# Low halves of the input projection's weight chunks 4 to 14: from VectorE to GpSimd

## The reference

```
h = rmsnorm(x, norm1_g) * (1 + sc1) + sh1
q_m, k_m, v_m, o_m, gate_m, conv_in, cq_raw, ckv_raw, krope = split_in(h @ p['w_in'])
y_m = mlstm_mixer(...)      # chunkwise matrix memory, forward and backward
y_c = conv_module(...)      # gated, then a depthwise convolution 31 wide, LayerNorm, pointwise
y_a = attention over latent queries and keys (8 heads)
x = x + g1 * (concat(y_m, y_c, y_a) @ p['w_out'])
x = x + g2 * ffn(rmsnorm(x) ...)
```

## Time and profile before

| | |
|---|---|
| median of 3 runs | 3638.81 us |
| profiled execution | 3644.04 us, its span 3642.20 us |
| PE busy | 3385.1 us (93%) |
| DVE busy | 1878.8 us (52%) |
| ACT busy | 864.7 us (24%) |
| POOL busy | 321.7 us (9%) |
| mean granted clock of TensorE | 0.95 of full |

### The profile page before, as it was taken

One profiled execution on the slowest core, in us unless ns is written; L12 is line 12 of the kernel. 1 busy time (PEld: TensorE's weight loads), 2 busy tenths in 40 slices (PEclk: granted clock), 3 DMA queues, 4 the chain that ended last, 5 costly groups with the idle time before them and its releaser, 6 DMA issues. The chain is left out here.

```text
span 3642.2 us, 45449 instructions
## 1 busy us (share of the span) xinstructions
PE 3385.1 (93%) x18642; PEld 3020.9 (83%) x18642; DVE 1878.8 (52%) x3068; ACT 864.7 (24%) x1332; POOL 321.7 (9%) x276
## 2 busy tenths in 40 slices
PE   5989989999899999999989896999997999999998
PEld 4988856557789999999979885655586999999998
DVE  6694644444666556565366655444415434433343
ACT  3212334444221111011132223344422111111100
POOL 0000111222110000000010001122121000000000
PEclk7996879999999999999999888899998999999999
DMA  5210100003322222122021000000110111111111
GB/s 246 88 32 1 62 4 4 3 12 122 106 75 76 86 75 81 63 83 80 28 87 45 18 3 16 2 4 3 45 66 32 50 35 46 35 46 46 46 35 53
DMA packets 44805, 185.60 MB, mean 51 GB/s; under 512 B 5440, under 2 KB 8960, under 8 KB 43136
## 3 DMA queue, kind: packets, MB, share of 16 engines
q1 hardware_dynamic: 37760, 158.58, 12.5%
q0 software_dynamic: 6912, 25.17, 2.4%
HBM read 169.14 MB, written 14.59 MB: 50 GB/s over the span
## 5 line engine op out<-in xcount | busy, mean ns | idle before, releaser
L1103 PE MATMUL ps<-a_hi,gu_hi 128*128 128x384 f32 x2112 | 711.9, 337 | 30.4 <-DVE a_lo L1630 24.2
L1103 PE MATMUL ps<-a_lo,gu_hi 128*128 128x384 f32 x2112 | 710.1, 336 | 0.0
L1103 PE MATMUL ps<-a_hi,gu_lo 128*128 128x384 f32 x2112 | 710.0, 336 | 0.0
L1103 PEld LDWEIGHTS ps<-a_hi,gu_hi 128*128 128x128 f32 x2112 | 400.0, 189 | 36.8 <-issue 18.0
L1103 PEld LDWEIGHTS ps<-a_lo,gu_hi 128*128 128x128 f32 x2112 | 400.1, 189 | 0.0
L1103 PEld LDWEIGHTS ps<-a_hi,gu_lo 128*128 128x128 f32 x2112 | 400.0, 189 | 0.0
L1132 PE MATMUL ps<-g_hi,d_hi 128*128 128x384 f32 x1056 | 354.3, 336 | 4.3 <-DVE g_lo L2081 4.3
L2079 DVE TENSOR_TENSOR at<-ps,sg 128x384 f32<-128x384 f32 x132 | 73.4, 556 | 545.9 <-ACT sg L1511 545.9
L1132 PE MATMUL ps<-g_lo,d_hi 128*128 128x384 f32 x1056 | 354.2, 335 | 0.0
L1132 PE MATMUL ps<-g_hi,d_lo 128*128 128x384 f32 x1056 | 353.9, 335 | 0.0
L1980 DVE TENSOR_REDUCE pmx<-ps 128x1 f32<-128x384 f32 (+1 forms) x400 | 213.4, 543 | 235.5 <-PE ps L1003 235.2
(11 more groups left out here) (261 smaller groups left out, 5095.2 us busy)
## 6 DMA issues: line engine op xcount, KB each, us to landing
f_raw<-wgu SPq DMA_DIRECT2D x88, 512.0 KB, 4.4
diag<-wada_c POOLq DMA_DIRECT2D x48, 512.0 KB, 3.8
f_raw<-wdn SPq DMA_DIRECT2D x44, 512.0 KB, 4.4
w_raw<-win SPq DMA_DIRECT2D x32, 512.0 KB, 3.6
spill<-z SPq DMA_DIRECT2D x2, 4608.0 KB
z<-spill SPq DMA_DIRECT2D x2, 4608.0 KB, 13.6
w_raw<-wout SPq DMA_DIRECT2D x16, 512.0 KB, 4.0
wada_o<-wada_b SPq DMA_DIRECT2D x16, 512.0 KB, 3.7
```

What stands on the lines that cost most here:

```text
L1103: mm = MM(ps[:, 2 * (v % 2) + part, 0:BLK], w, a[:, k, b * BLK:(b + 1) * BLK], start=(k == 0 and j == 0), stop=(k == KC - 1 and j == 2))
```

## The change

Eleven calls of `w_low` leave VectorE's list and stand as a loop in GpSimd's, behind its `a_lo` and in front of its `kw`. Chunks 0 to 3 and 15 stay on VectorE. The same subtraction is made on the same operands, with the same semaphores.

```diff
@@ VectorE
                 gated(0)
                 if l == 0:
                     late_modulation(0, 2)
-                w_low(4)
                 if l == 0:
                     late_modulation(2, 5)
-                w_low(5)
                 gated(1)
...
                 taps(0, 4)
-                w_low(6)
                 taps(4, 7)
                 kr_rows(0)
-                w_low(7)
                 dve.wait_ge(ml_reset.sem, ml_reset.at(l, 16))
                 gates()
                 scans(fw, False)
                 kr_rows(1)
-                w_low(8)
                 scans(bw, True)
                 row_maxima()
-                w_low(9)
                 row_offsets()
                 kr_rows(2)
                 taps(7, 9)
-                w_low(10)
                 taps(9, 13)
-                w_low(11)
                 taps(13, 17)
-                w_low(12)
                 taps(17, 21)
-                w_low(13)
                 taps(21, 22)
                 dve.wait_ge(ml_dmm.sem, ml_dmm.at(l, 1))
...
                 taps(22, 26)
-                w_low(14)
                 taps(26, CONV_WIDTH)
@@ GpSimd
                 low_halves(0)
+                for n in range(4, 15):
+                    w_low(n)
```

## The result

The changed kernel takes 3718.55 us, the median of four runs (3715.46 to 3721.61), and the kernel before, beside it, 3638.88 us (3636.89 to 3642.09). The ratio is 1.0218, with a 95% interval from 1.0200 to 1.0236. The forecast of 3633.9 us and its range are wrong. It came out as the fourth rival said, which gave about 3700 us and had a chance of 0.02.

A forecast was written before the change was run, and what follows sets the result against it. TensorE is 93% busy, but VectorE's chain was taken to end the stage; 2.44 us gained a layer, 4.9 us in both, turns 3644.04 into 3639.1, or 3633.9 us on the median's footing 5.2 us lower. Range 3628 to 3641.

The forecast's parts named there:

- the fourth rival: GpSimd doesn't get in between VectorE's instructions; chunk 10's low half comes 30 us late in each layer, about 3700 us; chance 0.02.
- Chunks 7 and 8 start without their wait: TensorE in the projection: each chunk's start falls from 2.11 to 0.36 us behind the transposes, 3.50 us a layer.
- It had first waited for the VectorE instruction in flight and then ran at the next boundary: GpSimd's `kw` beside a VectorE tap: it got in at the first boundary, taking 1.64 instead of 0.61 us.
- Done with 6 us to spare: GpSimd low halves in the projection: even one that first waits for a tap finishes 6 us before its chunk starts.
- A hold costs 2.2 us: Each GpSimd low half beside VectorE work with two SBUF inputs blocks VectorE for 2.2 us; five before `dcol`, one behind.
- the first rival: GpSimd's holds of VectorE cost next to nothing; the chain ends 4.64 us earlier a layer, 3629.5 us; chance 0.13.
- The third rival: VectorE becomes the bound before `dcol`; at 3.56 us a hold, the chain ends 4.8 us late a layer, 3648.5 us; chance 0.05.
- VectorE arrives 0.9 us before `dcol`, and the chain ends 2.44 us earlier: VectorE reaches `dcol` at 241.37, TensorE's matmuls at 242.26; VectorE's chain ends at 270.39 instead of 272.83 in layer 0.
- TensorE's wait for the value copies grows to 13.9 us: TensorE's idle time before the value transposes grows from 12.85 to about 13.9 us.
- The spread of the clock, 1.7 us a layer: Behind TensorE's long wait its half-speed clock may recover sooner or later: 1.7 us a layer, 3.4 us in all, either way.
- The fifth rival: TensorE's 27 us stretch at clock 0.98 stays at half speed: 13.5 us lost a layer, 3661 us in all; chance 0.03.

The follow-up runs named there:

- the first two experiments: First: changed kernel with only chunks 7 and 8's halves on GpSimd, 3633.53 us. Second: kernel before, those two halves earlier on VectorE, 3632.69 us.
- the second experiment: Kernel before with all low halves on VectorE, those of chunks 7 and 8 placed before the rope key row copies: 3632.69 us, ratio 0.9978.
- the four drains: Changed kernel with VectorE waiting for its own last tap behind taps 8, 12, 16 and 20 of the run: 3642.55 us timed, ratio 0.9998.
- chunk 14 moved: Kernel before with chunks 7 and 8's low halves earlier on VectorE and chunk 14's behind the first mask addition: 3646.73 us, ratio 1.0010.
- the third experiment: Changed kernel with chunk 10's low half back on VectorE, behind tap 8 of the run: 3679.80 us.
- the set moments: Changed kernel with GpSimd asking for chunks 10 to 13's halves after a chosen tap's end and a memset: 3720.47 us.
- the early requests: Changed kernel with four VectorE waits for its own last tap, GpSimd asking for chunks 10 to 13 right after taps 2, 9, 18, 26: 3644.04 us.

## Why the prediction was wrong, step by step

**Chunks 7 and 8 start without their wait: right.** No wait of TensorE for them is left in the changed kernel nor in the first two experiments, the `krt` copy that had stood at 178.42 stands at 176.20, and in the second experiment `dcol` comes 3.6 us earlier, counted from chunk 2's first matmul (3.50 in the forecast). What the experiments add is that GpSimd was not needed for it.

**"It had first waited for the VectorE instruction in flight and then ran at the next boundary": this is the step that failed.** It was read from a single `kw` beside a tap and carried to every low half. In the changed kernel chunk 10's half lost 30 instructions in a row. "Done with 6 us to spare" fell with it: the wait of 41.17 us (43.53 - 2.36) is nearly seven times the slack. The other outcome stood in the rows, an `a_lo` of 4.92 us behind two whole VectorE instructions, and was priced rightly at 30 us a layer. It was given 0.02 because the `kw` looked like the nearer case. Both rows were true of the same engines, which should have read as an unknown of that size. That the outcome matches the fourth rival's 3700 us means that this mechanism was seen and wrongly set aside.

**A hold costs 2.2 us: right, where GpSimd gets in.** A held tap takes 3.59 us instead of 1.44 (as at 276.63 above; 3.48 to 3.59 four times in the drained kernel), up to 2.15 us more. The scans on 4 partitions, of which the first rival said that they may not be held, are held as much: 4.62 us at 165.83, where the same scan takes 2.55 before, and 2.54 at 178.99 instead of 0.39. The third rival's "thrown out of step" did not occur.

**VectorE arrives 0.9 us before `dcol`, and the chain ends 2.44 us earlier: right once GpSimd gets in, and hidden in the changed kernel.** With the four drains VectorE idles 0.62 us, and in the first of its two profiled executions, from chunk 2's first matmul (100.10; 100.54 before) to the value transposes (272.41; 275.43 before) it takes 172.31 instead of 174.89 us, 2.6 us less. In the second it takes 173.88 us in layer 0, where the granted clock stands at 0.57 in the first 4 us of chunk 2 (1.00 in the first execution), and 172.33 in layer 1.

**TensorE's wait for the value copies grows to 13.9 us: right.** It is 13.86 us in the changed kernel and with the four drains.

**The spread of the clock, 1.7 us a layer: a term that was mis-sized.** It measured 5.6 and 5.7 us in the changed kernel's two layers, 5.3 and 5.9 with chunk 14 moved, and 5.5 and 3.0 with the drains. That is about two to three and a half times what was allowed. It isn't simply tied to the length of TensorE's wait: with chunk 14 moved the wait is shorter than before, with the drains longer, and both lose, while the third experiment has the wait of 13.86 us too and from there to the `hw` wait takes 148.50 us, as before. The fifth rival named the mechanism, at the wrong size (13.5 us).

## What to carry to other kernels

Before work goes to GpSimd beside a long back-to-back run of VectorE instructions with two SBUF inputs, price the case that it gets in only when the whole run is over, and ask who waits for it then. A single row in which it got in is no bound. Look first at the order of the list that makes the work late: here moving two calls one place up on the same engine gave 0.2%, as much as the best version with GpSimd. And a few us gained in front of a stretch at half clock can be lost in it, so read the granted clock behind the edit before counting them.

## What the runs showed of the hardware that was not expected

- GpSimd's subtraction stayed out for 30 VectorE instructions (41 us) in the changed kernel and for 27 with the set moments, and for 5 in the changed kernel's layer 1 (chunk 6's half, 8.97 us at 1975.93), while VectorE ran at its undisturbed pitch. So a wait here isn't bounded by one instruction.
- A wait of VectorE for its own last instruction let GpSimd in each time that a half was waiting there: chunk 10's in every kernel with drains, in both layers, and chunk 12's with the early requests. A drain costs about 0.1 us (the 8.96 us above, less 8.5 us for the four held taps, over four). Of the seven later requests in layer 0 behind these drains, three to six taps into the run, six got in at the first boundary.
- Open: what decides the first boundary. The moment within a tap doesn't (0.69 us shut out, 0.70 us served; 0.21 us served twice and refused twice). How VectorE came into the run fits all cases but two: chunk 12 with the early requests, and chunk 6 in layer 1, behind a drain as well and shut out until the taps ended. That VectorE's instructions in queue keep the access while they overlap is a likely story, but argued only.
- Behind TensorE's wait of 11 to 14 us the same work takes 148.2 to 148.6 us in some kernels and 153.6 to 154.1 in others, and in layer 1 of the kernels with drains 151.0 to 151.1, by a longer part at the lower clock (0.78 and 0.73 on average over the 120 us shown above). What selects it stays open.
